# PEER block and attention-FFN block on one core: weights' products on ScalarE, merged expert search, ScalarE sums for rows 132 to 191, a VectorE loop from row 192

## The reference, cut to what matters

```python
q = (hf @ w_q).reshape(T, 8, 2, 128)
s = einsum('thpd,hpnd->thpn', q, sub_keys)       # 128 scores for each half of each head
sv, si = top_k(s, 16)
cand = sv[:, :, 0, :, None] + sv[:, :, 1, None, :]
cand_idx = si[:, :, 0, :, None] * 128 + si[:, :, 1, None, :]
cv, ci = top_k(cand.reshape(T, 8, 256), 16)
expert = take_along_axis(cand_idx..., ci)         # 8 heads x 16 experts a token
g = softmax(cv)
u, vv = u_tab[expert], v_tab[expert]              # 16384 experts, rows of 1024 + 1024
a = gelu(einsum('cd,chkd->chk', x, u))
out = einsum('chk,chkd->cd', g * a, vv)
```

## Time and profile before

| | us |
|---|---|
| median of 3 runs | 1158.3 |
| lowest, highest | 1157.09, 1158.39 |
| the profiled execution | 1157.23 |
| its span, first to last instruction | 1155.4 |
| busy: TensorE, VectorE, ScalarE, GpSimd | 1030.7, 822.3, 431.8, 291.5 |
| gather queue, share of 16 DMA engines' span | 56.3% |

### The profile page before, as it was taken

The page is one execution under the profiler, slowest core; times in us unless marked ns, Lnnn a source line. Parts: engine busy times, 40 slices in busy tenths (PEclk is TensorE's granted clock), DMA queues, the critical chain, the costliest instruction groups (busy, mean ns, idle before and its releaser), DMA issues.

```text
span 1155.4 us, 13155 instructions
## 1 busy us (share of the span) xinstructions
PE 1030.7 (89%) x4830; PEld 675.3 (58%) x4830; DVE 822.3 (71%) x1892; ACT 431.8 (37%) x907; POOL 291.5 (25%) x262
## 2 busy tenths in 40 slices
PE   6999999999999887696877878878799999999997
PEld 3798977544344333342333433323299978999986
DVE  6787886877676776878878645555576878887843
ACT  3465733323233222233221211111365666565631
POOL 0000002445445443353444454444000000000000
PEclk9999999999999999998889898999999999999999
DMA  9988697999999999999999999999885354555440
GB/s 379 424 353 320 252 389 292 399 421 421 421 421 421 422 421 421 421 419 414 415 421 422 420 422 421 422 422 421 333 346 195 134 183 163 191 194 186 180 146 37
DMA packets 48337, 390.07 MB, mean 338 GB/s; under 512 B 5514, under 2 KB 6034, under 8 KB 7316
## 3 DMA queue, kind: packets, MB, share of 16 engines
q0 software_dynamic: 37040, 269.51, 56.3%
q1 hardware_dynamic: 11236, 119.77, 26.5%
HBM read 388.20 MB, written 1.06 MB: 337 GB/s over the span
## 4 chain that ended last, share of the span: by engine, by line
PE 56%; DMA 28%; DVE 11%; ACT 2%; issue 1%; POOL 1%; SPq 0%; DVEq 0%; ACTq 0%; POOLq 0%
DMA ring<-in_uv,idx 26%; PE ps L1672 17%; PE ps L2104 11%; PE ps L2085 7%; PE ps L2264 5%; PE ps L1697 2%; DVE ring L1458 2%; DMA ring<-in_w_ada 2%; PE ps L1853 2%; PE ps L1960 2%; PE ps L2192 2%; DVE ring L1010 1%; POOL ring L569 1%; DVE ring_r L999 1%; PE ps L1752 1%
## 5 line engine op out<-in xcount | busy, mean ns | idle before, releaser
L1458 DVE CUSTOM_DVE_ANT_0 ring<-h2t,ring 128x1024 f32<-128x1024 f32 x247 | 299.7, 1223 | 174.1 <-DMA ring<-in_uv,idx 174.0
L569 POOL DMA_INDIRECT ring<-in_uv,idx x247 | 278.5, 1128 | 329.5 <-PE ps L2104 152.3
L2085 PE MATMUL ps<-ring,probT 128*128 128x512 f32 x480 | 231.7, 640 | 61.7 <-ACT probT L866 61.7
L2104 PE MATMUL ps<-ring,probT 128*128 128x512 f32 x508 | 238.6, 606 | 35.6 <-ACT probT L866 35.5
L2085 PEld LDWEIGHTS ps<-ring,probT 128*128 128x128 f32 x480 | 95.7, 204 | 197.0 <-issue 110.7
L1672 PE MATMUL ps<-util_r,ring_r 128*128 128x256 f32 x1120 | 192.8, 282 | 0.3 <-ACT util L595 0.3
L2104 PEld LDWEIGHTS ps<-ring,probT 128*128 128x128 f32 x508 | 93.1, 192 | 157.2 <-issue 98.3
L999 DVE TENSOR_TENSOR ring_r<-ring,ring_r 128x1024 fp32r<-128x1024 f32 (+1 forms) x134 | 155.5, 1203 | 34.8 <-ACT ring_r L591 34.8
L861 ACT ACTIVATE prob<-prob 128x2 f32<-128x2 f32 (+2 forms) x98 | 20.0, 204 | 383.8 <-DVE prob L1458 383.8
L1672 PEld LDWEIGHTS ps<-util_r,ring_r 128*128 128x128 f32 x1120 | 158.1, 188 | 1.3 <-issue 0.7
L591 ACT ACTIVATE ring_r<-ring 128x1024 fp32r<-128x1024 f32 (+1 forms) x134 | 132.0, 1039 | 37.8 <-PE ps L2264 19.1
(11 more groups left out here) (298 smaller groups left out, 1072.3 us busy)
## 6 DMA issues: line engine op xcount, KB each, us to landing
ring<-in_w_in SPq DMA_DIRECT2D x11, 2048.0 KB, 13.7
ring<-in_w_up SPq DMA_DIRECT2D x11, 2048.0 KB, 8.0
ring<-in_w_ada SPq DMA_DIRECT2D x7, 2048.0 KB, 9.2
ring<-in_w_down SPq DMA_DIRECT2D x6, 2048.0 KB, 8.1
ring<-in_w_ada SPq DMA_DIRECT2D x8, 1024.0 KB, 13.8
ring<-in_w_out SPq DMA_DIRECT2D x4, 2048.0 KB, 9.2
ring<-in_w_q SPq DMA_DIRECT2D x3, 2048.0 KB, 12.1
ring<-in_w_in SPq DMA_DIRECT2D x4, 1024.0 KB, 10.1
```

Of the source, the lines that this page charges most:

```text
L569: e.indirect_dma_start(out=row_buf[n], out_offset=None, in_=uv, in_offset=bass.IndirectOffsetOnAxis(ap=idx[:, tt, k:k + 1], axis=0)).then_inc(
L1458: e.tensor_tensor_reduce(u, h2t[:, tt, :], u, 1.0, 0.0, ALU.mult, ALU.add, av[:, tt, n % 128:n % 128 + 1]).then_inc(*made.put(("dot", n)))
L2085: ins = e.matmul(acc[half][:, :], diag[:, (first + j) % DIAGS, :], row_buf[first + j][:, D + half * 512:D + (half + 1) * 512], start=False ...
L2104: ins = e.matmul(acc[half][:, :], diag[:, n % DIAGS, :], row_buf[n][:, D + half * 512:D + (half + 1) * 512], start=(k == 0), stop=(k == 127))
```

## The change

- `gate_exp` takes the exponentials head by head, each with its sum as an accumulated output; the sum on VectorE goes.
- The product of gelu and gate moves from VectorE to ScalarE, one column per row, with the gate as the activation's scale. The diagonals wait for ScalarE's own product.
- In `route` the conversions of positions go, the two tables of half numbers are scaled in one operation by a new constant `places` (128 and 1), and sums, comparison, pick, sum and copy are made for both heads at once. There are still 17 steps. Rows wait for the index copy of their whole group of heads.
- For rows 132 to 191 VectorE only multiplies; ScalarE adds up the 1024 products by a copy with an accumulated output.
- From row 192 to 251 VectorE's dot products run in a loop of 12 rows; each pass waits on a register's value, and the results go to 12 columns of `av` in turn (`dot_at`).
- The split of the turned third input moves from rows 204 and 208 to 184 and 188.

```diff
@@ -29,7 +29,7 @@
...
-CONST = dict(ident=128, ones=128, iota=16, eps=1, eps5=1, one=1, cmask=384, cosr=32, sinr=32)
+CONST = dict(ident=128, ones=128, iota=16, eps=1, eps5=1, one=1, places=2, cmask=384, cosr=32, sinr=32)
 COLS = dict(b_ada=48, g_mix=8, pscale=4, g_ffn=8, g_fin=8, ln1g=8, ln1b=8, ln2g=8, ln2b=8,
@@ -63,6 +63,8 @@
...
 DIAGS = 12
+SUMMED = range(132, 192)
+DOT_LOOP = (192, 252)
 ROW_LOOPS = {132: 180, 180: 252}
@@ -548,7 +550,7 @@
...
                 b, had = ROW_BUFS[n]
-                pool.wait_ge(made, ("idx", tt, k // 16) if n >= 8 else "first idxs" if n else "first idx")
+                pool.wait_ge(made, ("idx", tt, GROUP_OF[tt, k // 16]) if n >= 8 else "first idxs" if n else "first idx")
                 if had is not None:
@@ -575,6 +577,10 @@
...
                         sums.rearrange("(o h) t -> o (h t)", o=1).broadcast_to([P, 8 * T])).then_inc(*spread_sums.put("in"))
+        def dot_at(n):
+            return DOT_LOOP[0] % 128 + (n - DOT_LOOP[0]) % DIAGS if n >= DOT_LOOP[0] else n % 128
@@ -821,9 +827,11 @@
             def gate_exp(tt, h0, nh):
-                g3 = gw[:, tt, 16 * h0:16 * (h0 + nh)]
                 act.wait_ge(made, ("gate diff", tt, h0))
-                e.activation(g3, g3, ACT.Exp).then_inc(*acted.put(("gate exp", tt, h0)))
+                for h in range(h0, h0 + nh):
+                    g = gw[:, tt, 16 * h:16 * h + 16]
+                    ins = e.activation(g, g, ACT.Exp, accum_out=mx[:, 32 + h - h0:33 + h - h0])
+                ins.then_inc(*acted.put(("gate exp", tt, h0)))
@@ -852,15 +860,29 @@
...
                     row_root(3, 0)
-                if b0 == 204:
+                if b0 == 184:
                     act.wait_ge(made, ("gw", 1, 7))
...
                 ga = wt[:, tt, k0:k0 + size]
+                for n in range(b0, b0 + size):
+                    if n in SUMMED:
+                        u = row_buf[n][:, 0:D]
+                        act.wait_ge(made, ("dot", n))
+                        e.activation(u, u, ACT.Copy, accum_out=av[:, tt, n % 128:n % 128 + 1]).then_inc(
+                            *acted.put(("dot", n)))
+                if b0 in SUMMED:
+                    act.wait_ge(acted, ("dot", b0 + size - 1))
                 act.wait_ge(made, ("dot", b0 + size - 1))
-                e.activation(ga, av[:, tt, k0:k0 + size], ACT.Gelu).then_inc(*acted.put(("gelu", b0)))
+                at = dot_at(b0)
+                e.activation(ga, av[:, tt, at:at + size], ACT.Gelu).then_inc(*acted.put(("gelu", b0)))
+                act.wait_ge(acted, ("gelu", b0))
+                act.wait_ge(made, ("gw", tt, GROUP_OF[tt, k0 // 16]))
+                for k in range(k0, k0 + size):
+                    e.activation(wt[:, tt, k:k + 1], wt[:, tt, k:k + 1], ACT.Copy, scale=gw[:, tt, k:k + 1]).then_inc(
+                        *acted.put(("weight", 128 * tt + k)))
                 for n in range(b0, b0 + size):
-                    act.wait_ge(made, ("weight", b0))
+                    act.wait_ge(acted, ("weight", n))
                     if n >= DIAGS:
@@ -1337,47 +1359,43 @@
...
                 cand2 = mem[:, 2 * a:3 * a].rearrange("p (j n) -> p j n", j=nh)
-                hot = mem[:, 0:512].rearrange("p (k z n) -> p k z n", k=16, z=2)
-                both = [P, 16, 2, 16]
+                hot = mem[:, 0:512 * nh]
                 dve.wait_ge(acted, ("scores", h0 + nh - 1, tt))
...
                 dve.wait_ge(made, (*key, "s", "at2", 2 * nh - 1))
-                e.tensor_copy(sif[:, 0:2 * nh, :], si[:, 0:2 * nh, :]).then_inc(*made.put((*key, "si")))
-                for h in range(nh):
-                    e.tensor_tensor(cand[:, h, :].rearrange("p (a c) -> p a c", a=16),
-                                    sv4[:, h, 0, :].unsqueeze(2).broadcast_to([P, 16, 16]),
-                                    sv4[:, h, 1, :].unsqueeze(1).broadcast_to([P, 16, 16]), ALU.add).then_inc(
-                        *made.put((*key, "cand", h)))
+                e.tensor_tensor(si4[:, 0:nh], si.rearrange("p (h z) n -> p h z n", z=2)[:, 0:nh],
+                                K("places").unsqueeze(1).unsqueeze(3).broadcast_to([P, nh, 2, 16]), ALU.mult).then_inc(
+                    *made.put((*key, "si")))
+                every = [P, nh, 16, 16]
+                e.tensor_tensor(cand.rearrange("p h (a c) -> p h a c", a=16),
+                                sv4[:, 0:nh, 0, :].unsqueeze(3).broadcast_to(every),
+                                sv4[:, 0:nh, 1, :].unsqueeze(2).broadcast_to(every), ALU.add).then_inc(
+                    *made.put((*key, "cand")))
                 yield
-                dve.wait_ge(made, (*key, "cand", nh - 1))
+                dve.wait_ge(made, (*key, "cand"))
                 yield from top16((*key, "c"), nh, cv, ci, cand, cand2)
...
                     *made.put((*key, "col")))
+                yield
                 dve.wait_ge(made, (*key, "col"))
-                e.tensor_copy(pos[:, 0:nh, :, :], ch[:, 0:nh, :, :]).then_inc(*made.put((*key, "pos")))
-                e.tensor_scalar(si4[:, 0:nh, 0, :], si4[:, 0:nh, 0, :], 128.0, None, ALU.mult).then_inc(
-                    *made.put((*key, "si 128")))
-                dve.wait_ge(made, (*key, "si 128"))
-                for h in range(nh):
-                    yield
-                    if h > 0:
-                        dve.wait_ge(made, (*key, "picked", h - 1))
-                    e.tensor_tensor(hot[:, :], pos[:, h, :, :].unsqueeze(3).broadcast_to(both),
-                                    K("iota").unsqueeze(1).unsqueeze(1).broadcast_to(both), ALU.is_equal).then_inc(
-                        *made.put((*key, "hot", h)))
-                    dve.wait_ge(made, (*key, "hot", h))
-                    e.tensor_tensor(hot[:, :], hot[:, :], si4[:, h, :, :].unsqueeze(1).broadcast_to(both),
-                                    ALU.mult).then_inc(*made.put((*key, "pick", h)))
-                    dve.wait_ge(made, (*key, "pick", h))
-                    if nh == 1:
-                        yield
-                    e.tensor_reduce(ex[:, h, :], hot.rearrange("p k z n -> p k (z n)"), AX.X, ALU.add).then_inc(*made.put((*key, "picked", h)))
-                dve.wait_ge(made, (*key, "picked", nh - 1))
-                for h in range(h0, h0 + nh):
-                    e.tensor_copy(idx[:, tt, 16 * h:16 * h + 16], ex[:, h - h0, :]).then_inc(*made.put(("idx", tt, h)))
+                e.tensor_tensor(hot.rearrange("p (k n) -> p k n", n=16),
+                                ch[:, 0:nh].rearrange("p h k z -> p (h k z)").unsqueeze(2).broadcast_to([P, 32 * nh, 16]),
+                                K("iota").unsqueeze(1).broadcast_to([P, 32 * nh, 16]), ALU.is_equal).then_inc(
+                    *made.put((*key, "hot")))
+                dve.wait_ge(made, (*key, "hot"))
+                each = hot.rearrange("p (h k n) -> p h k n", h=nh, k=16)
+                e.tensor_tensor(each, each, si4[:, 0:nh].rearrange("p h z n -> p h (z n)").unsqueeze(2).broadcast_to(
+                    [P, nh, 16, 32]), ALU.mult).then_inc(*made.put((*key, "pick")))
+                yield
+                dve.wait_ge(made, (*key, "pick"))
+                found = ex[:, 0:nh, :].rearrange("p h k -> p (h k)")
+                e.tensor_reduce(found, hot.rearrange("p (k n) -> p k n", n=32), AX.X, ALU.add).then_inc(
+                    *made.put((*key, "picked")))
+                dve.wait_ge(made, (*key, "picked"))
+                e.tensor_copy(idx[:, tt, 16 * h0:16 * (h0 + nh)], found).then_inc(*made.put(("idx", tt, h0 + nh - 1)))
                 yield
@@ -1390,8 +1408,6 @@
...
                 dve.wait_ge(acted, ("gate exp", tt, h0))
-                e.tensor_reduce(mx[:, 32:32 + nh], g3, AX.X, ALU.add).then_inc(*made.put((*key, "total")))
-                dve.wait_ge(made, (*key, "total"))
                 e.reciprocal(mx[:, 40:40 + nh], mx[:, 32:32 + nh]).then_inc(*made.put((*key, "share")))
@@ -1431,6 +1447,17 @@
...
                     *made.put(("x low", n, tt, half)))
+            def looped_dots(first, end):
+                with e.Fori(0, 16 * (end - first) // DIAGS, 16) as more:
+                    for n in range(first, first + DIAGS):
+                        u, at = row_buf[n][:, 0:D], dot_at(n)
+                        e.wait_ge(arrived[n].sem, more + arrived[n].of(n))
+                        e.tensor_tensor_reduce(u, h2t[:, 1, :], u, 1.0, 0.0, ALU.mult, ALU.add,
+                                               av[:, 1, at:at + 1]).then_inc(made.sem, made.step)
+                for n in range(first, end):
+                    made.put(("dot", n))
@@ -1447,21 +1474,25 @@
...
                     x3_again(0)
-                if b0 == 208:
+                if b0 == 188:
                     for half in range(2):
                         turned_low(3, hi_r, lo_r, 0, half)
+                if b0 == DOT_LOOP[0]:
+                    looped_dots(*DOT_LOOP)
+                if DOT_LOOP[0] <= b0 < DOT_LOOP[1]:
```

(12 more changed lines are left out.)

## The result

| | before | changed |
|---|---|---|
| median of 7 runs, us | 1158.3 (1156.85 to 1158.84) | 1154.3 (1153.65 to 1155.32) |
| profiled execution, us (span) | 1157.23 (1155.4) | 1154.77 (1153.0) |
| last row landed (all 16 of its landings), us | 833.05 | 830.41 |

The ratio of the times is 0.9971 (95% interval 0.9962 to 0.998): by it 3.4 us gained, 1154.9 us for a kernel before of 1158.3. Two more measurements of the changed kernel, each beside the kernel before on the same chip, gave 0.9972 (0.9962 to 0.9983) and 0.9966 (0.9952 to 0.9979). The forecast was 1157.0, a gain of 1.3, in a range of 1154.8 to 1159.6: the time by the ratio lies just inside it, the median of the seven runs just outside. What came is on the side of case A, and the sign that was set for A, a last landing more than 2.5 us earlier, came too (2.64). The two profiled executions differ by 2.46 us.

The account below looks back on a forecast made before the run. Transfers of gathered expert rows, at about 421.5 GB/s, were taken as the bound beside the changed work. -0.33 - 1.03 + 0.24 = -1.1 us from the median 1158.3 gave 1157.2, taken as 1157.0, range 1154.8 to 1159.6.

Parts of the forecast that it names:

- case A: Rival: the transfer hole at 208 us closes too and the run-to-run excess may go; 1155.0 us, chance 0.27.
- the sign that was set for A: At the end of the gathers: a last landing more than 2.5 us earlier.
- Nothing else of size is lost between 188 and 826 us: Gathers: transfer holes at 492, 544 and 208 us are all a faster VectorE or earlier diagonal can win, 2.98 us.
- The terms -0.33 and -1.03: Gathers: earlier diagonals close the transfer holes at 492 to 496 us (0.33 us) and 544 to 556 us (1.03 us).
- The loop at 0: Looped dot products from row 192: same passes, VectorE idle time and 9.4 us of queueing cover them; 0 us.
- ScalarE's sums at 0: Rows 132 to 191: VectorE's pass hardly changes, ScalarE gains 1.14 us a row but keeps up; no gain of its own.
- Shorter searches: Routing: fewer and merged operations on VectorE, 5.3 us in all, beside the transfers and so worth nothing.
- the product off VectorE: Weights on ScalarE: four products take 0.88 us, diagonals come 1.06 us after gelu; pays only by helping close transfer holes.
- The end at +0.24: Last row: with the weight product on ScalarE, the diagonal and all that follows come 0.24 us later, bounds 0 to 0.5.
- the hole at 208 us: Transfers, 208 to 216 us: it stays since TensorE is busy throughout; 0 to 1.62 us gained, taken as 0.
- B: Rival: ScalarE frees the gather buffers late in rows 132 to 191, and the kernel is slower; 1161.3 us, chance 0.08.
- C: Rival: VectorE's dot-product loop stalls, delaying row 252 on leaving it; 1160 us, chance 0.05.

Follow-up runs that it names:

- e1: Kernel before, with VectorE's product of weights moved ahead of its batch's routing steps, instruction count unchanged; ratio to before 1.0002.
- e4: Changed kernel without its loop, the dot products of rows 192 to 251 written out; ratio to before 0.9986, where the changed kernel has 0.9966 to 0.9972.
- e5: Changed kernel without ScalarE's sums, dot products of rows 132 to 191 summed on VectorE again; ratio to before 0.9986, changed kernel 0.9972 on the same chip.
- e6: Changed kernel with ScalarE's sums in range(60, 180), loop from row 180, and 80 one-column VectorE copies at 14.8 us; ratio to before 1.0029.
- e3: Kernel before with 240 one-column copies on ScalarE, two behind each diagonal of rows 132 to 251; ratio to before 1.0002.
- e8: Changed kernel with ScalarE's sums in range(60, 180) and the loop from row 180, without extra copies; ratio to before 0.9964, changed kernel 0.9966.
- e2: Kernel before with 240 one-column copies on VectorE, two behind each dot product of rows 132 to 251; ratio to before 1.0023, 2.7 us slower.

## Why the forecast fell short

- **The number is near by luck.** The two terms that were to gain, 1.36 us in all, gained nothing (e1), and what did gain stood in the sum at 0.
- **The failed step** is "Nothing else of size is lost between 188 and 826 us. That is all that a faster VectorE or an earlier diagonal can win: 2.98 us." The windows' GB/s are a mean over 16 DMA engines. A row needs all of them, and the slowest had no hole at 492 or 544 us: it was 4.7 to 5.8 us behind the first one there. Across the hole of 544 us (rows 138 to 145) the first landings of a row fall back by 1.0 us, just what the forecast counted, and the last ones only by the 0.97 of the slip behind VectorE's fetch at 542.6, which is there in e1 without the hole too. What was lost stood in no window: 0.97 us for each of VectorE's fetches once its DMA engine is the last one, which is six times before the change and three times after it.
- **The terms -0.33 and -1.03** are worth 0. The holes closed by the mechanism forecast (diagonals 3.0 us earlier behind the last product where 2.7 was worked out), and e1 closed them without any gain.
- **The loop at 0** is worth one slip (e4). The argument was about stalls of VectorE, and there were none: row 252, the first behind the loop, starts at 823.06 after 1.25 us of waiting for its row. What the loop saves is a fetch that holds up the slowest DMA engine. The Trainium skill (Runtime: NRT & Kernel Launch, "Instruction fetch mechanics") calls the price of going on to the next block of instructions mostly hidden, and counts branches against a kernel. Here VectorE's own time agrees with "hidden", but the last landing comes 0.97 us later for each fetch, and the loop is a gain.
- **ScalarE's sums at 0** (VectorE's pass 1.220 us for 1.223) were right for the passes and wrong for the time: one instruction a row less on VectorE is worth a slip (e5). The dot product, told above as one instruction, is two in the trace, the pass and a read of its sum of 0.08 us; a pass without a sum is one.
- **"Shorter searches" and the product off VectorE** at 0: fewer instructions too. e4 and e5 lose 1.6 us or more each of 3.4, so by the ratios little is left for these; by the slips it is one of three. They were not run alone.
- **The end at +0.24** was +0.13: gelu to diagonal is 0.56 us where it was 0.43, because ScalarE's wait for its own result is 0.03 to 0.04 (from 831.90 to 831.93, from 832.22 to 832.26), not the 0.09 of the earlier trace rows.
- **Right:** the sums at 1.13 to 1.14 us a row, the weights at 0.85 for four, ScalarE's 117 us, the hole at 208 us. B did not come: from 560 to 700 us every stretch of 20 us stays at 421 or 422 GB/s. C did not come.

Groups of the changed kernel by form, 186 to 836 us (busy us, mean ns, idle before), behind the last three points:

```profile
L1457 DVE CUSTOM_DVE_ANT_0 ring<-h2t,ring 128x1024 f32<-128x1024 f32 x60 | 73.7, 1228 | 75.0 <-DMA ring<-in_uv,idx 75.0
L1491 DVE TENSOR_TENSOR ring<-h2t,ring 128x1024 f32<-128x1024 f32 x60 | 71.9, 1220 | 38.0 <-DMA ring<-in_uv,idx 37.9
L872 ACT ACTIVATE ring<-ring 128x1024 f32<-128x1024 f32 x60 | 63.2, 1053 | 35.8 <-DVE ring L1491 35.5
L882 ACT ACTIVATE prob<-prob 128x1 f32<-128x1 f32 x256 | 58.3, 285 | 3.2
```

**Open:** why a fetch of VectorE costs 0.97 us and one of ScalarE 0.6 to 0.7. Where the lateness of the slowest DMA engine at the start comes from: row 12 is complete at 221.0 to 223.1 us from run to run (e6 left out), which may be why the ratio gives 3.4 us and the profiled executions 2.46. In four traces (before, changed, e3, e8) it is late by 1.3 to 1.5 us just behind a 16 KB fetch of TensorE; the rest is open. That VectorE's and ScalarE's fetches ride on one and the same DMA engine each time is read from ranks and steps, not from a name in the records. And how the three slips divide over the parts, to better than one slip.

## What to carry to other kernels

Where gathers keep all DMA engines busy, read when a row's last part lands and not the mean GB/s: closing a hole of the mean won nothing here (e1). Then count the instructions of the engine whose fetches ride on the slowest DMA engine: 240 tiny ones on an engine with time to spare cost 2.7 us (e2), and a loop wins although that engine is busy for only 432 of 644 us. A long stage is the place for this, since each fetch shifts everything that follows it.

## What the runs showed of the hardware that I had not expected

VectorE and ScalarE fetch instructions in 8 KB pieces, 128 instructions each; TensorE's are 16 KB (0.57 MB in 35), outside the loops one for some 127 matmuls with their weight loads. They show in the landings too: behind the one at 219.6 us row 12 is 1.34 us late in the kernel before (1.41 to 1.53 in the changed kernel, e3 and e8), and behind another row 50 is 1.44 us late in e3. From row 90 on only one of them moved the last landings, in e6. The pieces go through DMA engines that also carry the gathers: 0.97 us for one of VectorE's and 0.6 to 0.7 for one of ScalarE's, on two different DMA engines, though the piece is 8 KB and a gathered row's part on one engine is 1.053 MB / 16 = 66 KB in 2.49 us, by which 8 KB would be 0.3 us; the fetch's own packet takes that long (0.7% of 16 engines in 3 us, 0.34 us). Where the other 0.6 us go is not shown. Between the fastest and the slowest DMA engine 7.4 us build up in 256 rows.
